# Down projection by seven block products instead of eight, with the sums of weight blocks made in DRAM

## What is computed

```python
h2 = rms_norm(x, g_ffn_pre[i])
u = causal_dwconv(h2 @ w_up[i], conv_w[i], conv_b[i])
ug, uv = u[..., :D_FF], u[..., D_FF:]
f = (jax.nn.gelu(ug, approximate=True) * uv) @ w_down[i]      # (512 x 2816) @ (2816 x 1024)
x = x + rms_norm(f, g_ffn_post[i])

pg = jax.nn.sigmoid(rms_norm(x, g_ple_pre[i]) @ w_ple_gate[i])
x = x + rms_norm(pg * (p[i] @ w_ple[i]), g_ple_post[i])
```

## Time and profile before

| | |
|---|---|
| time, median of 3 runs | 1843.96 us |
| the profiled execution, first to last instruction (span) | 1842.0 us |
| PE, matmuls | 1833.6 us busy, 100% |
| PE, weight loads | 1528.1 us, 83% (they overlap matmuls) |
| DVE | 1038.2 us, 56% |
| ACT | 884.6 us, 48% |
| POOL | 164.1 us, 9% |
| DMA engines | 34.2% of 16 engines' span, mean 100 GB/s |
| granted TensorE clock, mean | 0.999 |

### The profile page before, as it was taken

How to read it: one execution, slowest core, us unless ns; L and a number is a source line. 1 busy time by engine, 2 the same in 40 slices (tenths; PEclk the granted TensorE clock), 3 DMA queues, 4 the chain that set the end, 5 groups by cost and what they waited for, 6 DMA issues and landing times.

```text
span 1842.0 us, 26192 instructions
## 1 busy us (share of the span) xinstructions
PE 1833.6 (100%) x9243; PEld 1528.1 (83%) x9243; DVE 1038.2 (56%) x1658; ACT 884.6 (48%) x1552; POOL 164.1 (9%) x178
## 2 busy tenths in 40 slices
PE   9999999999999999999999999999999999999998
PEld 8888888788888888888898888887888888888887
DVE  4756555545577767324656565555445777763244
ACT  4676546533454444224547764465335444442253
POOL 1002000011011111001010020001111111110010
PEclk9999999999999999999999999999999999999999
DMA  6322353234323333323243224532342333333322
GB/s 184 77 81 84 106 106 95 61 95 161 103 81 102 91 101 93 125 92 97 85 148 88 64 83 112 104 93 64 95 168 81 103 91 102 91 102 115 103 81 80
DMA packets 280164, 183.66 MB, mean 100 GB/s; under 512 B 62564, under 2 KB 262912, under 8 KB 279808
## 3 DMA queue, kind: packets, MB, share of 16 engines
q1 hardware_dynamic: 279688, 182.13, 34.2%
q10 hardware_dynamic: 376, 0.21, 0.1%
HBM read 175.68 MB, written 4.46 MB: 98 GB/s over the span
## 4 chain that ended last, share of the span: by engine, by line
PE 99%; DVE 0%; ACT 0%; issue 0%; DVEq 0%; POOL 0%; POOLq 0%; ACTq 0%
PE psum L791 89%; PE psum L1022 2%; PE psum L1003 2%; PE psum L988 2%; PE psum L834 1%; PE psum L975 1%; PE psum L974 1%; PE psum L1000 0%; PE psum L985 0%; PE psum L1212 0%; PE psum L984 0%; PE psum L803 0%; PE psum L820 0%; PE psum L1272 0%; DVE xnl L1743 0%
## 5 line engine op out<-in xcount | busy, mean ns | idle before, releaser
L791 PE MATMUL psum<-xnh,wh 128*128 128x512 f32 (+1 forms) x1424 | 563.8, 396 | 0.0
L791 PE MATMUL psum<-xnh,wl 128*128 128x512 f32 (+1 forms) x1424 | 548.6, 385 | 0.0
L791 PE MATMUL psum<-xnl,wh 128*128 128x512 f32 (+1 forms) x1424 | 548.0, 385 | 0.0
L1729 DVE TENSOR_TENSOR wl<-raw,wh 128x1024 fp32r<-128x1024 f32 (+1 forms) x272 | 355.1, 1306 | 292.9 <-ACT wh L1330 292.8
L1330 ACT ACTIVATE wh<-raw 128x1024 fp32r<-128x1024 f32 (+1 forms) x272 | 284.0, 1044 | 363.7 <-PE psum L791 349.1
L791 PEld LDWEIGHTS psum<-xnh,wl 128*128 128x128 f32 x1424 | 267.5, 188 | 54.6
L791 PEld LDWEIGHTS psum<-xnh,wh 128*128 128x128 f32 x1424 | 269.0, 189 | 50.4 <-issue 2.7
L791 PEld LDWEIGHTS psum<-xnl,wh 128*128 128x128 f32 x1424 | 268.2, 188 | 46.7
L1854 DVE CUSTOM_DVE_ANT_0 Sp<-psum,ptok 128x128 f32<-128x128 f32 (+3 forms) x128 | 62.7, 491 | 108.7 <-issue 61.7
L791 PE MATMUL psum<-wh,fh 128*128 128x512 f32 x288 | 112.0, 389 | 0.0
L791 PE MATMUL psum<-wh,fl 128*128 128x512 f32 x288 | 112.0, 389 | 0.0
(11 more groups left out here) (281 smaller groups left out, 2901.2 us busy)
## 6 DMA issues: line engine op xcount, KB each, us to landing
raw<-in_w_up_dram SPq DMA_DIRECT2D x88, 512.0 KB, 3.7
raw<-in_w_gate_dram SPq DMA_DIRECT2D x48, 512.0 KB, 3.7
raw<-in_w_down_dram SPq DMA_DIRECT2D x44, 512.0 KB, 3.5
raw<-in_w_in_dram SPq DMA_DIRECT2D x30, 512.0 KB, 3.9
raw<-in_w_out_dram SPq DMA_DIRECT2D x16, 512.0 KB, 3.5
raw<-in_w_ple_gate_dram SPq DMA_DIRECT2D x16, 512.0 KB, 4.2
rx<-rspill SPq DMA_DIRECT2D x48, 128.0 KB, 2.9
raw<-in_w_in_dram SPq DMA_DIRECT2D x16, 260.0 KB, 3.0
```

The source lines that it names most:

```text
L791: ins = pe.matmul(out, left, right, start=start and n == 0, stop=stop and n == 2)
L1729: dve.tensor_tensor(low[:, 0:n], raw[(L * NCH + c) % RAW][:, 0:n], hi[:, 0:n].bitcast(F32), ALU.subtract).then_inc(w_lo.sem, 1)
```

## The change

The output is divided in two by token halves (blocks 0, 1 against 2, 3) and in two by column halves (0 to 511, 512 to 1023). The inner dimension is divided in two by even and odd feature tiles. The eight products of such blocks are replaced by seven products of sums and differences of blocks. Each of the seven is 256 tokens x 1408 features x 512 columns: 11 pairs of tiles x 2 token blocks x 3 matmuls = 66 matmuls.

- **Weights.** A pair of feature tiles (2j, 2j+1) now needs four chunks: `dn_raw` (two corners of the raw weights), `dn_rows` (sum of the even and the odd row tile), `dn_cols` (sum of the two column halves) and `dn_diff` (two other corners, of which DVE makes a difference in place). Round one takes `dn_raw` and `dn_rows` of all 11 pairs, for products two, five, three and four, 12 matmuls a chunk. Round two takes `dn_cols` (products six and seven, 12 matmuls) and `dn_diff` (product one, 6 matmuls). These are 44 chunks of 512 KB in place of 22. I number them n = 0 to 43 in the order of loading.
- **Sums of weights in DRAM.** At the start of each layer POOL issues two plain transfers of 5.77 MB each from `w_down` into `row_sums` and `col_sums`, waits for them, and issues two adding transfers of the same size (`weight_sums`).
- **Features.** POOL makes, for each pair, the difference `f_cross` and three half-tile differences `f_sums` (128x768), and SP stores the latter into DRAM (`qspill`, 384 KB a pair). During the down projection SP fetches them back into `q_raw`, two buffers, and ACT and DVE split them into `qh` and `ql`. The fetches stand in SP's queue behind the loads of chunks n = 9, 11, ... 21 (pairs 0 to 6) and 29, 31, 33, 35 (pairs 7 to 10).
- **Between the rounds** ACT copies products two and five out of PSUM, and DVE combines them with three and four. After round two DVE adds products six, one and seven and goes on to the residual.
- **Slots.** High and low parts have four slots in the down projection (two lie where the up projection's input was), and six further ones for the last three pairs.

The core of the diff (first version `-`, changed `+`):

```diff
+PAIRS = FT // 2
+CHUNKS += [(k, j) for j in range(PAIRS) for k in ("dn_raw", "dn_rows")]
+CHUNKS += [(k, j) for j in range(PAIRS) for k in ("dn_cols", "dn_diff")]
...
+DN_TAIL = 3
+DN_SLOTS = 4
+Q_PREP = [2 * j + 6 for j in range(7)] + [26, 28, 30, 32]
...
         def load(L, c):
             moves = chunk_dmas(L, c)
             wait(w_lo.sem, w_lo.at(L, c - RAW + 1))
+            if CHUNKS[c] == ("dn_rows", 0):
+                wait(wsum_in.sem, wsum_in.at(L, 32))
...
+                for j in range(PAIRS):
+                    if c == ST_UP + 4 * j + 11:
+                        wait(q_ready.sem, q_ready.at(L, j + 1))
+                        sp.dma_start(qspill[L, :, j, :], f_sums[:, :]).then_inc(q_spilled.sem, 16)
+                    if c == ST_DOWN + Q_PREP[j] + 3:
+                        if j == 0:
+                            wait(f_lo.sem, f_lo.at(L, 3 * PAIRS))
+                        wait(q_spilled.sem, q_spilled.at(L, 16 * PAIRS) if j == 0 else q_spilled.at(L, 16 * (j + 1)))
+                        if j >= 2:
+                            wait(q_lo.sem, q_lo.at(L, j - 1))
+                        sp.dma_start(q_raw[j % 2][:, :], qspill[L, :, j, :]).then_inc(q_back.sem, 16)
...
             elif c in EXTRA:
                 act.wait_ge(w_used.sem, w_used.at(L, c - EXTRA[c] - 2))
+            elif c in DN_NEAR:
+                act.wait_ge(w_used.sem, w_used.at(L, max(c - DN_SLOTS + 1, ST_DOWN)))
+            elif c in DN_LATE:
+                pair = (4 * DN_LATE[c] + 3) // 3
+                act.wait_ge(w_used.sem, w_used.at(L, ST_DOWN + 2 * PAIRS + 2 * pair + 2))
...
+        def sums_hi(L, j):
+            act.wait_ge(q_back.sem, q_back.at(L, 16 * (j + 1)))
+            act.wait_ge(w_used.sem, w_used.at(L, ST_DOWN + 2 * j + 2))
+            act.activation(qh[:, j, :], q_raw[j % 2][:, :], ACT.Copy).then_inc(q_hi.sem, 1)
...
+        def down_chunks(L):
+            for n in range(3, 4 * PAIRS + 2):
+                hi(L, ST_DOWN + n)
+                if n in Q_PREP:
+                    sums_hi(L, Q_PREP.index(n))
+                if n == 2 * PAIRS + 1:
+                    products_out(L)
+                if n == 31:
+                    half_sums(L)
...
             hi(L, ST_DOWN + 1)
+            hi(L, ST_DOWN + 2)
             up_post(L, -1, 2 * FT // 4)
-            for c in range(ST_DOWN + 2, ST_PG):
-                hi(L, c)
-            for t in range(TB):
-                y_sum(L, 1, t, wide_of[t], sq_down)
-                if t > 0:
-                    x_sum(L, 2, t - 1, sq_down)
+            cross_hi(L, PAIRS - 1)
+            down_chunks(L)
+            for i in range(TB):
+                rest_sum(L, i)
+                if i > 0:
+                    x_sum(L, 2, DN_ORDER[i - 1], sq_dn)
             ple_out(L, ST_PLE)
...
+        def diff(L, j):
+            s = (L * NCH + ST_DOWN + 2 * PAIRS + 2 * j + 1) % RAW
+            dve.wait_ge(w_landed[s], LAND[L * NCH + ST_DOWN + 2 * PAIRS + 2 * j + 1])
+            dve.tensor_tensor(raw[s][:, 0:512], raw[s][:, 0:512], raw[s][:, 512:1024], ALU.subtract
+                              ).then_inc(diff_made.sem, 1)
...
+        def down_chunks(L):
+            for n in range(3, 4 * PAIRS):
+                q = n - 2 * PAIRS
+                if q >= 0 and q % 2 == 0:
+                    diff(L, q // 2)
+                if n == 2 * PAIRS + 2:
+                    threes_taken(L, 0)
+                    threes_taken(L, 1)
+                lo(L, ST_DOWN + n)
+                if n == 2 * PAIRS + 3:
+                    fours_taken(L, 0)
+                    fours_taken(L, 1)
+                if n in Q_PREP:
+                    sums_lo(L, Q_PREP.index(n))
+                if n in (33, 34, 35, 36):
+                    half_gain(L, n - 33)
...
+        def weight_sums(L):
+            rows = A["w_down"].rearrange("l (j m p) c -> l m p j c", m=2, p=P)
+            cols = A["w_down"].rearrange("l (t p) (h c) -> l h p t c", p=P, h=2)
+            pool.dma_start(row_sums[L], rows[L, 0]).then_inc(wsum_copied.sem, 16)
+            pool.dma_start(col_sums[L], cols[L, 0]).then_inc(wsum_copied.sem, 16)
+            pool.wait_ge(wsum_copied.sem, wsum_copied.at(L, 32))
+            pool.dma_start(row_sums[L], rows[L, 1], accum_op=ALU.add).then_inc(wsum_in.sem, 16)
+            pool.dma_start(col_sums[L], cols[L, 1], accum_op=ALU.add).then_inc(wsum_in.sem, 16)
```

More of the change, by code:

```diff
@@ L80 @@
 ST_DOWN = len(CHUNKS)
-CHUNKS += [("down", j) for j in range(FT)]
+PAIRS = FT // 2
+CHUNKS += [(k, j) for j in range(PAIRS) for k in ("dn_raw", "dn_rows")]
+CHUNKS += [(k, j) for j in range(PAIRS) for k in ("dn_cols", "dn_diff")]
 ST_PLE = len(CHUNKS)
@@ L88 @@
 SPL = 2
-TAIL = {"out": 4, "down": 4, "pg": 6}
+TAIL = {"out": 4, "pg": 6}
 EXTRA = {}
-for _s, _n in ((ST_OUT, KT), (ST_DOWN, FT), (ST_PG, KT)):
+for _s, _n in ((ST_OUT, KT), (ST_PG, KT)):
     for _e in range(TAIL[CHUNKS[_s][0]]):
@@ L94 @@
 EXTRA.update({2: 0, 3: 1})
-RING = [c for c in range(NCH) if c not in EXTRA]
+DN_TAIL = 3
+DN_SLOTS = 4
+DN_TAIL_AT = 4 * PAIRS - 2 * DN_TAIL
+DN_NEAR = {ST_DOWN + n: n % DN_SLOTS - SPL for n in range(DN_TAIL_AT) if n % DN_SLOTS >= SPL}
+DN_LATE = {ST_DOWN + n: n - DN_TAIL_AT for n in range(DN_TAIL_AT, 4 * PAIRS)}
+RING = [c for c in range(NCH) if c not in EXTRA and c not in DN_NEAR and c not in DN_LATE]
 assert len(RING) % SPL == 0
@@ L107 @@
 FW = 340
-WIDTH = {"first": 2 * FW}
+WIDTH = {"first": 2 * FW, "dn_diff": 512}
 F_GATE, F_PE, F_VC = 512, 520, 552
-G_OF = {"first": 0, "out": 0, "down": 0, "pg": 0, "uqn": 2, "uqp": 2, "ukn": 0, "ukv": 4, "ple": TB,
+G_OF = {"first": 0, "out": 0, "dn_raw": 0, "dn_rows": 0, "dn_cols": 0, "dn_diff": 0, "pg": 0, "uqn": 2, "uqp": 2, "ukn": 0, "ukv": 4, "ple": TB,
         "branch0": 2, "branch1": 2, "branch2": 2}
@@ L611, in chunk_dmas @@
             return [(v(KT), w_up[L, :, :, col:col + P])]
-        if kind == "down":
-            return [(full, w_down[L, :, m, :])]
+        if kind in ("dn_raw", "dn_diff"):
+            corners = bass.AP(tensor=A["w_down"].tensor, offset=(L * DFF + 2 * P * m) * D,
+                              ap=[[D, P], [P * D + D // 2, 2], [1, D // 2]])
+            return [(full.rearrange("p (k c) -> p k c", k=2), corners)]
+        if kind == "dn_rows":
+            return [(full, row_sums[L, :, m, :])]
+        if kind == "dn_cols":
+            return [(full.rearrange("p (k c) -> p k c", k=2), col_sums[L, :, 2 * m:2 * m + 2, :])]
         if kind == "ple":
@@ L867, in turn_all @@
         def turn_all(L):
-            for t in range(1, TB):
-                block_free(L, 1, t)
+            pe.wait_ge(rest_made.sem, rest_made.at(L, TB))
             for t in range(TB):
@@ L1327, in hi @@
             s = (L * NCH + c) % RAW
-            act.wait_ge(w_landed[s], LAND[L * NCH + c] + it * 16)
+            if CHUNKS[c][0] == "dn_diff":
+                act.wait_ge(diff_made.sem, diff_made.at(L, CHUNKS[c][1] + 1))
+            else:
+                act.wait_ge(w_landed[s], LAND[L * NCH + c] + it * 16)
             n = width(c)
@@ new lines, in products_out, with half_sums @@
+        def products_out(L):
+            for k, dst in enumerate((p_two, p_five)):
+                for a in range(2):
+                    if (k, a) == (1, 1):
+                        act.wait_ge(w_used.sem, w_used.at(L, ST_DOWN + 2 * PAIRS - 1))
+                    else:
+                        act.wait_ge(p_full.sem, p_full.at(L, 2 * k + a + 1))
+                    act.activation(dst[a][:, :], bank[4 + 2 * k + a], ACT.Copy).then_inc(p_out.sem, 1)
+        def half_sums(L):
+            for i, t in enumerate((0, 1, 2, 3)):
+                act.wait_ge(half_made.sem, half_made.at(L, i + 1))
+                act.wait_ge(half_summed.sem, half_summed.at(L, i))
+                act.activation(sq_dn[0][:, early_half(t)], ydn[:, t, early_half(t)], ACT.Square, scale=YSCALE,
+                               accum_out=ysums[:, 0, t:t + 1]).then_inc(half_summed.sem, 1)
@@ L2213, in _ @@
             links[0] = after + 2
-            for c in range(ST_DOWN + 2, ST_PG):
+            down_chunks(L)
+            for c in range(ST_PLE, ST_PG):
                 lo(L, c)
-            residual(L, 1)
+            down_rest(L)
             lo(L, ST_PG)
```

374 lines of the change are left out of this document (302 added, 72 removed).

## The result

The changed kernel takes 2018.21 us (median of 4 runs, 2017.55 to 2019.0), the kernel before 1843.88 beside it: 1.0945 times as long, 95% interval 1.0929 to 1.096. The prediction was 1897 us with a range up to 1956. The direction was right, the size was not: 174.3 us slower in place of 53.

What follows compares the result with a forecast made beforehand. PE, busy for the whole span, was taken as the bound. Waits of 77.2 us, minus 29.9 for removed matmuls, plus 6 for weight sums, gave +53.3: 1897 us, own range 1868 to 1925, 8 in 10 from 1866 to 1956.

Steps and rivals of the forecast that it cites:

- Matmuls removed: Down projection: 66 fewer matmuls a layer at 0.2267 us each, a gain of 29.9 us for both layers.
- Round one and two: Down projection: one load-fetch-split loop takes 8.0 us against PE's 5.44 in round one, 7.4 against 4.08 in round two.
- The fit of 2.9 us: Down projection fetch: 2.0 us plus bytes over 436 GB/s, making the forecast about 30 us less; 4.25 us was taken.
- The small terms: Down projection waits a layer: 2.2 us before chunk 3, 1.8 in the first turn, 4.8 in the last three pairs.
- the entry: Start of the down projection: chunk 3 ready after 10.6 us, PE asks after 8.2, so PE waits 2.2 us.
- The term of the sum: Waits a layer: 19.4 us round one, 12.8 round two, 4.8 last three pairs, 1.6 residual, together 38.6.
- PE's clock falls: Rival, down projection: the clock halves in waits and PE becomes the bound, 23 us a layer, 1944 us; chance 0.06.
- The residual and the up projection: ACT's square of x delays the first ple bank, 1.6 us a layer; the up projection's extra work hides beside PE, 0.
- The weight sums: From the start of each layer: the sums' transfers beside the weight loads cost 3 us a layer, ends 0 and 30.
- queues that take turns by piece: Rival, start of each layer: engines alternate pieces, loads take 9 to 15 us, 30 us a layer, 1951 us; chance 0.13.
- The signs: 924 down-projection matmuls; PE waits some 70 us for DVE's low parts; ACT waits for 22 fetches; turns 8.0 and 7.4.
- the three signs of being wrong: Wrong if qh finds its tile landed, PE waits elsewhere (loads at 40 to 140 us), or granted clock is under 0.98.

Runs made afterwards that it cites:

- Experiment 5: Changed kernel without weight sums (chunks loaded from raw weights) and with each fetch but the first issued two chunks earlier: 1849.77 us.
- experiment 1: Changed kernel without weight sums, the chunks loaded from raw weights with the same bytes and row lengths: 1900.36 us.
- experiment 3: Changed kernel with the transfers of the weight sums cut by columns into rows of 512 B, same bytes: 1997.43 us.
- experiment 2: Changed kernel with the two adding transfers of a layer made plain copies of the same size: 1973.76 us.

## Why the prediction was wrong

**Matmuls removed, -29.9 us.** The count is exact. As a gain it exists only on paper until the waits are gone: without sums and with earlier fetches the kernel still takes 1849.8.

**Round one and two, 8.0 and 7.4 us a turn.** Right: 7.95 and 7.6 us measured, the fetch 4.4 us against 4.25. The fit of 2.9 us that the prediction set beside it stands in the Trainium skill (DMA: Bandwidth & Descriptors, Anatomy of one DMA) for transfers that GpSimd issues; SP issued these, and the trace does not agree with it. Experiment 5 took the loop away and 25 us a layer with it. The small terms were right too, as far as that run shows them: 2.3 us before chunk 3 and 2.2 before chunk 7 against 2.2 and 1.8, and 5.5 in the last three pairs against 4.8. The parts listed for the entry add up to 10.9 us and not 10.6; that changes nothing.

The term of the sum, 38.6 us a layer, came out at 29.0 + 15.0 = 44. PE stood still for less (29 us between 800 and 955), and the clock, which I had left at full, fell. The window of the changed kernel:

```profile
860.00:955.00 95.00, 76.33 (x292) 58.60 (x291) 60.33 (x74) 40.18 (x59) 3.30 (x7) 0.91 0.61 203
```

Where the supply sets the turn, a lower clock need not cost anything, since slower matmuls only fill the wait. In round one the turn from 859.4 to 867.1 us took 7.6 us with the clock at 0.79 (window 860 to 868), the one before 7.8 at 1.00. It costs in the chunks behind, where PE is the bound (0.81 from 940 to 955 us). Of the 15 us of the 44 that were not standing still, the clock can account for some 11, an estimate from the 0.93 granted between 800 and 955 us (0.07 x 155); the rest I did not separate. The rival "PE's clock falls" (23 us a layer, chance 0.06) had the fall right, and its consequence wrong: PE did not become the bound of the turns.

**The residual and the up projection, 1.6 and 0.** The up projection cost nothing without pieces: PE was busy 135 of 135 us in experiment 1. My cover for it, DVE's slack of 2 us, did hold, and was used up as soon as POOL issued transfers as well.

**The weight sums, 3 us a layer.** This is the step that failed: 60 us (59 by experiment 1), outside the ends of 0 and 30 that I gave the term. I had priced a load beside the sums at some 5 us, which the lead hides; the nine loads behind the start took 86.7 us in place of 33.4. The reason that I gave for the low value, "most of that stretch is attention, with fewer loads in a unit of time", was read from the whole 100 us. The loads that hurt are the nine right behind the start, 33.4 us for nine, one each 4.2 us. The rival "queues that take turns by piece" came nearest: its price for a load, 9 to 15 us, matches 9.8 and 16.4. How the engines divide their time between the queues no run shows cleanly (experiment 3). It counted 8 loads hit, as in the trace (8.3 in 108 us). What it had wrong was the other side: it subtracted 5.44 us that PE needs between loads, where they were needed each 4.2. With the measured numbers, 4.2 x 9.8 + 4.1 x 16.4 = 108 us, less 8.3 x 4.2 = 35, less 16 of lead, are 57 us a layer; with three chunks of lead at 4.2 us, 12.6, they are 61. Its range reached 60, but I took 30 and gave it 0.13. That an adding transfer takes 67 us where a copy takes 42 I had only as a condition ("if an adding transfer costs as a copy"), with no end for the other case; experiment 2 prices it at 22 us a layer.

**The signs.** ACT waited for the fetch 22 times, as forecast, and the matmuls are 132 fewer. By the table of waits PE waited 38 us for DVE's low parts (`dn_wl`, `wl`), in place of some 70. Two of the three signs of being wrong came: PE stood still for want of loads between 40 and 140 us, and the granted clock was 0.963.

The page of the Trainium skill that I held to leave both open (DMA: Bandwidth & Descriptors, Queues, rings and completion order: an engine takes its queues in turn, packet by packet) did point at the outcome. By that rule what counts is the size of a packet on either side. The trace agrees in the direction and not in the ratio: with both queues at work the loads got 1.6, 1.5 and 0.78 packets for one of the sums, and not 1, while the sums' packets went from 4.05 to 2.7 to 0.5 KB.

## What to carry over

- A background transfer is not priced by its bytes but by how long a needed load must share the engines with it: ask for the interval of the loads in the 50 us behind its start, not for the mean DMA share. Cut it into pieces of some 5 us, let one be under way at a time, and keep them away from small transfers that an engine waits for at once, and from an engine whose own work would be put off by issuing them.
- A fetch that stands behind a load in one queue, and ahead of that load's successor in the consumer's order, closes a loop whose length is the sum of all latencies in it. Moving the fetch two places up was worth 50 us and cost one line and a second semaphore.
- Fewer matmuls pay only if whatever feeds PE keeps up with the shorter time for each chunk. Here half the time for twice as many chunks left waits at the entry and the tail that ate the 30 us.

## What I had not expected of the hardware

- An adding transfer from DRAM to DRAM of 11.5 MB took 67 us beside loads, the same as a copy 42. In rows of 512 B it went at 115 GB/s, in rows of 2 and 4 KB at 172.
- The copies kept packets of 3.8 KB when their rows were cut to 512 B, and the adding transfers did not: 506 B. With rows of 2 and 4 KB the copies had 4.05 KB a packet and the adding transfers 2.7, about one row each (4224 rows, 4256 packets).
- POOL's subtraction stretched a DVE instruction from 0.75 to 2.27 us, and POOL's issue of a transfer alone (1 us for 512 KB) did not stretch it at all: 0.75 us three times.
- 16 matmuls without use kept the clock at 1.00 through waits in which it otherwise fell to 0.50, and the kernel was not faster for it.
